# Memory tokens staged in scratch, pass-0 activations loaded ahead of the K/V projection, four io buffers

## The chip, the cores and the metric

The kernel runs on all 8 cores of one Trainium2 chip. Each core works on its own share of the data with its own copy of the program, and no core talks to another. The metric is the device time in microseconds of the slowest core.

## The reference, cut to what matters

The reference is one layer of a decoder for two groups of requests that share weights. Each core has one prompt of 2048 tokens, 16 sample requests of 8 tokens (128 rows), and 256 memory tokens, all 1024 wide:

```
mn = rms(mem_prompt, g_mem); mk = mn @ w_xk; mv = mn @ w_xv     # 256 tokens, both are outputs too
x += 0.5 * swiglu(rms(x) ; w_ffn1_in, w_ffn1_out)
x += concat(pool(z), conv(z)) @ w_mix_out      with z = rms(x) @ w_mix_in
x += cross_attn(rms(x), mk, mv)                # sample rows use cached keys and values
x += 0.5 * swiglu(rms(x) ; w_ffn2_in, w_ffn2_out)
y  = rms(x)
```

## The kernel before

The activations live on chip in transposed form: `xT` holds 8 blocks of 128 features by 1152 token columns in f32. The 2048 prompt tokens are done in two passes of 1024 columns (subs 0 and 1, of 512 columns each). The 128 sample rows are sub 2, at columns 1024 to 1151; they take part in the first half of the layer in pass 0 and in the second half in pass 1. `hT` (bf16) holds the normed activations, `U` (bf16) the inner ones of the FFN and of the mixer. `scr` is f32 scratch. It is 4224 elements wide in each partition, in three parts that the program calls `R0`, `R1` and `R2`; the mixer, the sample attention and the final norm use it.

A small planner, `Prog.add`, puts every instruction into the list of its engine in the order in which the Python code emits it. It derives the waits from named resources: a reader waits for the last writer, a writer for earlier readers and writers on other engines. No engine reorders its own list, so an instruction that waits holds up everything that stands behind it on the same engine. Plain loads and stores are issued by SP, weight loads (f32 in memory, cast to bf16 on the way) by POOL. Both kinds run on the core's 16 DMA engines, as two queues: q1 for SP, q0 for POOL.

Weights go through four slots `wsl` in the order of use. `prefetch(3)` issues the first four blocks, the two halves of `w_xk` and of `w_xv`, ahead of everything else. A later block is issued when the matmuls that read its slot are done.

`load_tokens` (L399) brings in 128 tokens: SP loads a 128 x 1024 f32 tile, 512 KB, into one of two `io` buffers. TensorE transposes its eight blocks into two PSUM banks. ScalarE copies the first bank and VectorE the second into `xT`. The buffer is free for the next load when the transposes have read it.

The opening runs in this order on every engine: two memory tiles into columns 0 to 255 of `xT`; the norm with gain 3 into `hT`; the key projection to `kTp`; sixteen 128 x 512 halves of K and V as rows, of which eight groups of matmuls, each copied by ScalarE into one of two `stg` buffers (L446) and stored by SP (L451); three state loads through the same `stg` buffers, with transposes and copies to `poolhT` and `convhT` (L460 to L474); then eight tiles of `x_p` and one of `x_s` with `load_tokens`; then the first norm of FFN 1 (L305 the squares, L205 the sum over features with a matrix of ones, L313 and L315 the reciprocal root, L321 the scaling).

At the end of pass 0 the two subs are finished one after the other. For each, `final_sub` (L555) norms into `yT` in `scr` (gain 5), transposes four tiles of 128 tokens back, copies each into an `io` buffer (ScalarE L570, VectorE L572) and lets SP store it to `y_p` (L578). Then four tiles of the next pass are loaded with `load_tokens` into the same columns of `xT`, and their norm for FFN 1 follows. Output tiles and loads take the `io` buffers in turn. At the end of pass 1 `final_sub` runs for subs 0, 1 and 2 without loads.

Of the kernel before, what the change touches and what calls it, by code (L numbers as in the profile page):

```python
# [6 lines left out]
F32 = mybir.dt.float32  # L7
BF16 = mybir.dt.bfloat16
AF = mybir.ActivationFunctionType
# [6 lines left out]
EPS = 1e-6  # L16
# [96 lines left out]
def build_program(dbg_stage=None, skip=()):  # L113
# [29 lines left out]
    def sb(name, shape, dt):  # L143
        return es.enter_context(nc.sbuf_tensor(name, list(shape), dt))
# [5 lines left out]
    sq = sb("sq", [128, 8, 512], BF16)  # L150
    rstd = [sb(f"rstd{i}", [128, 512], F32) for i in range(2)]
    sg = [sb(f"sg{i}", [128, 512], F32) for i in range(2)]
    io = [sb(f"io{i}", [128, 1024], F32) for i in range(2)]
    scr = sb("scr", [128, 3 * 1408], F32)
    scr2 = sb("scr2", [128, 3 * 1408], F32)
    scr_bf = scr.bitcast(BF16)
# [37 lines left out]
    def nb():  # L194
        b = bank_ctr[0] % 8
        bank_ctr[0] += 1
        return b

    def BK(b):
        return ("ps", b)  # L200
# [57 lines left out]
    def wres(b, npart):  # L258
        return [("w", b % 4, pi) for pi in range(npart)]
# [37 lines left out]
    def XR(si, k):  # L297
        return ("x", si, k)
# [27 lines left out]
    def norm(src, subs, gi, dst_t):  # L326
        for sub in subs:
            r, rr, xr = norm_sub(src, sub, gi, dst_t)
            norm_apply(src, sub, gi, (lambda k, c0, n: dst_t[:, k, c0:c0 + n]), r, rr, xr, (lambda si: [("hT", si)]))
# [64 lines left out]

    io_ctr = [0]

    def load_tokens(src_rows_ap, col0, si):
        i = io_ctr[0] % 2
        io_ctr[0] += 1  # L399
        buf = io[i]  # L400
        P.add("sp", (lambda e: e.dma_start(out=buf[:], in_=src_rows_ap)), writes=[("io", i)], dma_key=f"io{i}")
        for half in range(2):
            b = nb()
            for j in range(4):
                k = half * 4 + j
                transp(ps[b][:, j * 128:(j + 1) * 128], buf[:, k * 128:(k + 1) * 128], identf[:], [("io", i)], b)
            dstv = xT[:, half * 4:half * 4 + 4, col0:col0 + 128]
            srcv = ps[b][:, :].rearrange("p (j t) -> p j t", j=4)
            eng = "act" if half == 0 else "dve"
            if eng == "act":  # L410
                P.add("act", (lambda e, dstv=dstv, srcv=srcv: e.activation(out=dstv, in_=srcv, func=AF.Copy)),
                      reads=[BK(b)], writes=[XR(si, half * 4 + j) for j in range(4)])
            else:
                P.add("dve", (lambda e, dstv=dstv, srcv=srcv: e.tensor_copy(out=dstv, in_=srcv)),  # L414
                      reads=[BK(b)], writes=[XR(si, half * 4 + j) for j in range(4)])

    SUB_P = [(0, 0, 512), (1, 512, 512)]
    SUB_S = [(2, 1024, 128)]

    prefetch(3)  # L420
    if "kv" not in skip:
        for mc in range(2):
            load_tokens(mem[mc * 128:(mc + 1) * 128, :], mc * 128, 0)
        if "kv_norm" not in skip:
            norm(xT, [(0, 0, 256)], 3, hT)
        xk = sched["xk"]; xv = sched["xv"]
        for oc in (range(8) if "kv_kt" not in skip else []):
            blk = xk[oc // 4]
            sv = slot_view_blk(blk, 8, 512)
            b = nb()  # L430
            mm_group(ps[b][:, 0:256], [(sv[:, k, (oc % 4) * 128:(oc % 4 + 1) * 128], hT[:, k, 0:256]) for k in range(8)],
                     wres(blk, 1) + [("hT", 0)], b)
            P.add("act", (lambda e, b=b, oc=oc: e.activation(out=kTp[:, oc, :], in_=ps[b][:, 0:256], func=AF.Copy)),
                  reads=[BK(b)], writes=["kTp"])
        stg_ctr = [0]
        for (wb, dst_d, is_v) in (((xk, nk_p, False), (xv, nv_p, True)) if "kv_tok" not in skip else []):
            for mc in range(2):
                for cb in range(2):
                    blk = wb[cb]
                    sv = slot_view_blk(blk, 8, 512)  # L440
                    b = nb()
                    mm_group(ps[b][:, :], [(hT[:, k, mc * 128:(mc + 1) * 128], sv[:, k, :]) for k in range(8)],
                             wres(blk, 1) + [("hT", 0)], b)
                    i = stg_ctr[0] % 2
                    stg_ctr[0] += 1
                    P.add("act", (lambda e, b=b, i=i: e.activation(out=stg[i][:, :], in_=ps[b][:, :], func=AF.Copy)),  # L446
                          reads=[BK(b)], writes=[("stg", i)])
                    if is_v and "kv_vp" not in skip:
                        P.add("dve", (lambda e, i=i, mc=mc, cb=cb: e.tensor_copy(out=Vp[:, mc, cb * 512:(cb + 1) * 512], in_=stg[i][:, :])),
                              reads=[("stg", i)], writes=["Vp"])  # L450
                    P.add("sp", (lambda e, i=i, dst_d=dst_d, mc=mc, cb=cb: e.dma_start(  # L451
                        out=dst_d[mc * 128:(mc + 1) * 128, cb * 512:(cb + 1) * 512], in_=stg[i][:, :])),
                        reads=[("stg", i)], dma_key=f"stg{i}")
# [102 lines left out]
    def final_sub(sub):  # L556
        (si, c0, n) = sub
        pss_ = cur_pass[0]
        r, rr, xr = norm_sub(xT, sub, 5, None)
        norm_apply(xT, sub, 5, (lambda k, c0_, n_: yT3[:, k, 0:n_]), r, rr, xr, (lambda si_: ["R0", "R1", "R2"]))  # L560
        for tcn in range(n // 128):
            i = io_ctr[0] % 2
            io_ctr[0] += 1
            for half in range(2):
                b = nb()
                for j in range(4):
                    k = half * 4 + j
                    transp(ps[b][:, j * 128:(j + 1) * 128], yT3[:, k, tcn * 128:(tcn + 1) * 128], identf[:], ["R0", "R1", "R2"], b)
                if half == 0:
                    P.add("act", (lambda e, b=b, i=i: e.activation(out=io[i][:, 0:512], in_=ps[b][:, :], func=AF.Copy)), reads=[BK(b)], writes=[("io", i)])  # L570
                else:
                    P.add("dve", (lambda e, b=b, i=i: e.tensor_copy(out=io[i][:, 512:1024], in_=ps[b][:, :])), reads=[BK(b)], writes=[("io", i)])  # L572
            if si < 2:
                r0 = pss_ * 1024 + c0 + tcn * 128
                dst = y_p[r0:r0 + 128, :]
            else:
                dst = y_s[:, :]
            P.add("sp", (lambda e, i=i, dst=dst: e.dma_start(out=dst, in_=io[i][:, :])), reads=[("io", i)], dma_key=f"io{i}")  # L578
# [8 lines left out]
    for pss in range(2):  # L587
        cur_pass[0] = pss
        subs_a = SUB_P + (SUB_S if pss == 0 else [])
        subs_b = SUB_P + (SUB_S if pss == 1 else [])  # L590
        if "load" not in skip and not (pss == 1 and preload_next):
            for tcn in range(8):
                r0 = pss * 1024 + tcn * 128
                load_tokens(x_p[r0:r0 + 128, :], tcn * 128, tcn // 4)
            if pss == 0:
                load_tokens(x_s[:, :], 1024, 2)
# [362 lines left out]
```

How the kernel before makes its waits and increments, by code:

```python
    def emit(self, eng, handle, esem, dsem, final_wait=False):  # L86
        waited = {}
        for o in self.ops[eng]:
            for d in o.deps:
                if d.dma_key is not None:
                    sem = dsem[d.dma_key]
                    if d.dma_key in self.wait_all_keys:
                        val = 16 * self.dma_count[d.dma_key]
                    else:
                        val = 16 * d.dma_idx
                else:
                    sem = esem[d.eng]
                    val = d.sig_val
                key = id(sem)
                if waited.get(key, 0) < val:
                    handle.wait_ge(sem, val)
                    waited[key] = val
            ins = o.fn(handle)
            if o.dma_key is not None:
                ins.then_inc(dsem[o.dma_key], 16)
            elif o.signal:
                ins.then_inc(esem[eng], 1)
        if final_wait:
            for k, cnt in self.dma_count.items():
                handle.wait_ge(dsem[k], 16 * cnt)
```

## Time and profile before

| | us |
|---|---|
| median of 2 timed runs (1764.76 to 1765.17) | 1764.97 |
| the profiled execution, its own time | 1759.95 |
| span of its slowest core, first to last instruction | 1758.4 |
| spans of the 8 cores | 1752.9 to 1758.4 |
| TensorE busy in that span | 1509.1 |
| share of TensorE in the chain that ended last | 78% |

The rows further down are all from the slowest core, core 7, of the profiled execution. Times in them are microseconds from the start of the span. PE is TensorE, PEld its weight loads, DVE is VectorE, ACT is ScalarE, POOL is GpSimd, and SPq is the queue that issues SP's DMAs. Brackets at the end of a row of the timeline give the idle time before the instruction and what ended it.

### The profile page before, as it was taken

How to read it: one execution, taken by the hardware profiler on the slowest of the kernel's cores; microseconds unless marked ns; L12 is line 12 of the kernel's file. 1: busy time of each engine (PE TensorE's matmuls, PEld its weight loads, DVE VectorE, ACT ScalarE, POOL GpSimd, SP SyncE). 2: the span in 40 equal slices, each digit the busy share in tenths (PEclk: the TensorE clock that was granted, in tenths of full speed). 3: DMA queues.
4: the chain of work that ended last, by engine and by line, in shares of the span. 5: the costliest groups of instructions: out<-in, count | busy, mean ns of one | idle time of the engine just before them, and what ended most of it. 6: DMA issues, size and time to landing. Idle time of an engine off the chain costs nothing.

```text
span 1758.4 us, 23002 instructions; the slowest of 8 cores (1752.9 to 1758.4 us)
## 1 busy us (share of the span) xinstructions
PE 1509.1 (86%) x8516; PEld 758.1 (43%) x8516; DVE 611.9 (35%) x1046; ACT 411.3 (23%) x631; POOL 158.0 (9%) x191
## 2 busy tenths in 40 slices
PE   5269999986988889999953799998698889999984
PEld 3135554543444335545532344443243345454533
DVE  1042323246551442323343222224554252323243
ACT  2131010123124433231312210112312522011122
POOL 1000010010000011111100000001000000010000
PEclk9659999998999989999986799999899989999996
DMA  8913363552353269898982165547163334475502
GB/s 144 185 61 49 48 97 49 77 53 28 51 89 52 28 90 133 117 144 112 145 159 80 46 80 74 72 61 78 18 91 55 48 44 52 48 86 60 61 1 108
DMA packets 175178, 135.01 MB, mean 77 GB/s; under 512 B 29485, under 2 KB 160685, under 8 KB 175070
## 3 DMA queue, kind: packets, MB, share of 16 engines
q0 software_dynamic: 167344, 111.29, 49.3%
q1 hardware_dynamic: 7726, 22.26, 3.7%
q8 instruction: 71, 1.16, 0.3%
q14 instruction: 37, 0.30, 0.1%
HBM read 233.21 MB, written 11.60 MB: 139 GB/s over the span
## 4 chain that ended last, share of the span: by engine, by line
PE 78%; DVE 7%; DMA 6%; ACT 6%; issue 3%; SPq 0%; DVEq 0%; ACTq 0%; POOLq 0%
PE ps L205 75%; PE ps L209 3%; ACT sq L305 2%; DMA io<-x_p 2%; DVE hT L321 2%; DVE scr L659 1%; DVE scr L321 1%; DMA y_p<-io 1%; ACT ET L829 1%; DMA nv_p<-stg 1%; DMA scr<-ck 1%; DVE scr L733 1%; DMA io<-mem 1%; ACT rstd L313 1%; DMA stg<-st_pool 0%
## 5 line engine op out<-in xcount | busy, mean ns | idle before, releaser
L205 PE MATMUL ps<-hT,wsl 128*128 128x512 bf16 (+2 forms) x4800 | 914.1, 353 | 16.4 <-DVE hT L321 11.2
L205 PEld LDWEIGHTS ps<-hT,wsl 128*128 128x128 bf16 x4800 | 437.9, 99 | 486.9 <-issue 48.0
L205 PE MATMUL ps<-U,wsl 128*128 128x512 bf16 (+1 forms) x2080 | 387.5, 348 | 7.1 <-DVE U L744 5.3
L385 DVE TENSOR_TENSOR U<-ps,sg 128x512 bf16<-128x512 f32 (+1 forms) x220 | 134.6, 612 | 489.4 <-PE ps L205 469.9
L205 PEld LDWEIGHTS ps<-U,wsl 128*128 128x128 bf16 x2080 | 186.4, 98 | 203.6 <-issue 10.0
L383 ACT ACTIVATE sg<-ps 128x512 f32<-128x512 f32 (+1 forms) x220 | 117.4, 533 | 656.7 <-PE ps L205 656.6
L341 DVE SCALAR_TENSOR_TENSOR xT<-ps,xT 128x512 f32<-128x512 f32 (+1 forms) x240 | 144.7, 611 | 169.3 <-PE ps L205 167.0
L205 PE MATMUL ps<-sq,ones_n 128*128 128x512 bf16 (+2 forms) x208 | 64.0, 473 | 72.1 <-ACT sq L305 58.9
L321 DVE SCALAR_TENSOR_TENSOR hT<-xT,gains_sb,rstd 128x512 bf16<-128x512 f32 (+2 forms) x168 | 97.9, 657 | 72.8 <-ACT rstd L315 72.8
L305 ACT ACTIVATE sq<-xT 128x4096 bf16<-128x4096 f32 (+2 forms) x26 | 79.3, 3051 | 94.8 <-DVE xT L345 56.3
L209 PE MATMUL ps<-identf,io 128*128 128x128 f32 x152 | 35.2, 412 | 48.1 <-DMA io<-x_p 34.2
L345 DVE TENSOR_TENSOR xT<-ps,xT 128x512 f32<-128x512 f32 (+1 forms) x80 | 47.6, 610 | 66.2 <-PE ps L205 66.2
L205 PEld LDWEIGHTS ps<-sq,ones_n 128*128 128x128 bf16 x208 | 22.8, 122 | 108.7 <-issue 101.0
L252 POOL DMA_DIRECT2D wsl<-w_f1i x44 | 38.5, 883 | 252.0 <-PE ps L205 251.7
L252 POOL DMA_DIRECT2D wsl<-w_f2i x44 | 38.5, 885 | 246.1 <-PE ps L205 245.7
L209 PE MATMUL ps<-identf,scr 128*128 128x128 f32 x136 | 24.2, 360 | 33.2 <-DVE scr L321 33.2
L209 PEld LDWEIGHTS ps<-identf,io 128*128 128x128 f32 x152 | 29.0, 217 | 53.3 <-issue 53.3
L840 DVE TENSOR_TENSOR hT<-ps,rstd 128x512 bf16<-128x512 f32 x32 | 20.6, 686 | 84.3 <-ACT rstd L835 84.3
L313 ACT ACTIVATE rstd<-ps 128x512 f32<-128x512 f32 (+2 forms) x26 | 13.7, 528 | 113.6 <-PE ps L205 113.6
L414 DVE COPY xT<-ps 128x512 f32<-128x512 f32 x19 | 13.1, 692 | 77.1 <-PE ps L209 77.1
L252 POOL DMA_DIRECT2D wsl<-w_f1o x12 | 10.3, 856 | 316.3 <-PE ps L205 316.3
L209 PEld LDWEIGHTS ps<-identf,scr 128*128 128x128 f32 x136 | 23.0, 194 | 36.1 <-issue 36.1
(106 smaller groups left out, 611.4 us busy)
## 6 DMA issues: line engine op xcount, KB each, us to landing
wsl<-w_f1i POOLq DMA_DIRECT2D x44, 512.0 KB, 8.6
wsl<-w_f2i POOLq DMA_DIRECT2D x44, 512.0 KB, 10.9
io<-x_p SPq DMA_DIRECT2D x16, 512.0 KB, 4.1
wsl<-w_f1o POOLq DMA_DIRECT2D x8, 1024.0 KB, 8.8
scr<-ck POOLq DMA_DIRECT2D x16, 512.0 KB, 8.8
scr<-cv POOLq DMA_DIRECT2D x16, 512.0 KB, 7.2
wsl<-w_f2o POOLq DMA_DIRECT2D x8, 1024.0 KB, 12.2
y_p<-io SPq DMA_DIRECT2D x16, 512.0 KB, 2.8
```

What stands on the lines that cost most here:

```text
L205: P.add("pe", (lambda e, l=l, r=r, i=i: e.matmul(out_ap, lhsT=l, rhs=r, start=(i == 0), stop=(i == n - 1))), reads=reads, writes=[BK(b)])
L209: P.add("pe", (lambda e: e.transpose(out_ap, in_ap, ident_ap)), reads=reads + ["c_identf", "c_identb"], writes=[BK(b)])
L252: batch.append(P.add("pool", (lambda e, dst=dst, src=src: e.dma_start(out=dst, in_=src.rearrange("(k p) n -> p k n", p=128))), writes=[("w ...
L305: P.add("act", (lambda e: e.activation(out=sq[:, :, 0:n], in_=src[:, :, c0:c0 + n], func=AF.Square)), reads=xr, writes=["sq"])
L313: P.add("act", (lambda e: e.activation(out=r[:, 0:n], in_=ps[b][:, 0:n], func=AF.Ln, bias=EPS, scale=1.0)), reads=[BK(b)], writes=[rr])
L321: P.add("dve", (lambda e, k=k: e.scalar_tensor_tensor(out=dst(k, c0, n), in0=src[:, k, c0:c0 + n], scalar=gains[:, gi, k:k + 1], in1=r[:, ...
L341: P.add("dve", (lambda e, b=b, o=o, c0=c0, n=n: e.scalar_tensor_tensor(out=xT[:, o, c0:c0 + n], in0=ps[b][:, 0:n], scalar=0.5, in1=xT[:, o ...
L345: P.add("dve", (lambda e, b=b, o=o, c0=c0, n=n: e.tensor_tensor(out=xT[:, o, c0:c0 + n], in0=ps[b][:, 0:n], in1=xT[:, o, c0:c0 + n], op=AL ...
L383: P.add("act", (lambda e, bg=bg, n=n, s_=s_: e.activation(out=s_[:, 0:n], in_=ps[bg][:, 0:n], func=AF.Silu)), reads=[BK(bg)], writes=[("sg ...
L385: P.add("dve", (lambda e, bu=bu, n=n, s_=s_, jl=jl, c0=c0: e.tensor_tensor(out=U[:, jl, c0:c0 + n], in0=ps[bu][:, 0:n], in1=s_[:, 0:n], op ...
L659: P.add("dve", (lambda e, srcb=srcb, dstb=dstb, lo=lo, kstep=kstep: e.tensor_tensor(out=dstb[:, lo:1039], in0=srcb[:, lo:1039], in1=srcb[: ...
L840: P.add("dve", (lambda e, bo=bo, c=c, c0=c0, n=n, r=r: e.tensor_tensor(out=hT[:, c, c0:c0 + n], in0=ps[bo][:, 0:n], in1=r[:, 0:n], op=ALU. ...
```

## The change

There are three edits.

1. The `io` buffers become four (`NIO = 4`), in `load_tokens` and in `final_sub`.
2. The memory tiles are transposed into `memT`, the first 2048 columns of `scr`, with resource `R0`. They are normed from there into `U`, and both projections read `U` in place of `hT`. The instructions of that norm are the same in number and size.
3. The nine loads of pass 0 with their transposes and copies are emitted directly behind the two memory tiles, ahead of the memory norm, and leave their old place behind the state loads.

```diff
-    io = [sb(f"io{i}", [128, 1024], F32) for i in range(2)]
+    NIO = 4
+    io = [sb(f"io{i}", [128, 1024], F32) for i in range(NIO)]
...
-    def load_tokens(src_rows_ap, col0, si):
-        i = io_ctr[0] % 2
+    def load_tokens(src_rows_ap, col0, si, dst3=None, res_of=None):
+        dst3 = xT if dst3 is None else dst3
+        res_of = (lambda k: XR(si, k)) if res_of is None else res_of
+        i = io_ctr[0] % NIO
...
+    early_x = all(k not in skip for k in ("kv", "load"))
     prefetch(3)
     if "kv" not in skip:
+        memT = scr[:, 0:2048].rearrange("p (k t) -> p k t", k=8)
         for mc in range(2):
-            load_tokens(mem[mc * 128:(mc + 1) * 128, :], mc * 128, 0)
+            load_tokens(mem[mc * 128:(mc + 1) * 128, :], mc * 128, 0, dst3=memT, res_of=(lambda k: "R0"))
+        if early_x:
+            for tcn in range(8):
+                load_tokens(x_p[tcn * 128:(tcn + 1) * 128, :], tcn * 128, tcn // 4)
+            load_tokens(x_s[:, :], 1024, 2)
         if "kv_norm" not in skip:
-            norm(xT, [(0, 0, 256)], 3, hT)
+            P.add("act", (lambda e: e.activation(out=sq[:, :, 0:256], in_=memT[:, :, :], func=AF.Square)), reads=["R0"], writes=["sq"])
...
+            for k in range(8):
+                P.add("dve", (lambda e, k=k, r=r: e.scalar_tensor_tensor(
+                    out=U[:, k, 0:256], in0=memT[:, k, :], scalar=gains[:, 3, k:k + 1], in1=r[:, 0:256], op0=ALU.mult, op1=ALU.mult)),
+                    reads=["R0", ("rstd", 0), "c_gains"], writes=[("U", 0)])
...
         for tcn in range(n // 128):
-            i = io_ctr[0] % 2
+            i = io_ctr[0] % NIO
...
-        if "load" not in skip and not (pss == 1 and preload_next):
+        if "load" not in skip and not (pss == 1 and preload_next) and not (pss == 0 and early_x):
```

## Rows read from the trace of the kernel before

**Rows 1.** The page, parts 1 and 4: busy share, and the chain by engine.

```profile
PE 1509.1 (86%) x8516; PEld 758.1 (43%) x8516; DVE 611.9 (35%) x1046; ACT 411.3 (23%) x631; POOL 158.0 (9%) x191
...
PE 78%; DVE 7%; DMA 6%; ACT 6%; issue 3%; SPq 0%; DVEq 0%; ACTq 0%; POOLq 0%
```

**Rows 2.** The timeline, 0 to 60 us: start, duration, engine, line, op.

```profile
3.38 0.90 SPq L401 DMA_DIRECT2D io<-mem  x2
...
15.10 1.94 PE L209 MATMUL ps<-identf,io 128*128 128x128 f32 x8 [0.95 <-DMA io<-mem]
...
17.93 1.91 ACT L305 ACTIVATE sq<-xT 128x2048 bf16<-128x2048 f32 x1 [1.05 <-DVE xT L414]
...
26.34 8.98 PE L205 MATMUL ps<-hT,wsl 128*128 128x256 bf16 x64 [4.49 <-DVE hT L321]
```

**Rows 3.** The timeline, 60 to 130 us.

```profile
71.76 25.25 SPq L401 DMA_DIRECT2D io<-x_p  x8
...
78.68 0.28 ACT L474 ACTIVATE convhT<-ps 128x128 f32<-128x128 f32 x1 [0.55 <-PE ps L209]
...
104.56 3.61 ACT L305 ACTIVATE sq<-xT 128x4096 bf16<-128x4096 f32 x1
```

**Rows 4.** DMA queues, 8 to 12 us: packets, MB, share of 16 engines.

```profile
q1 hardware_dynamic: 202, 0.76, 62.4%
q0 software_dynamic: 232, 0.24, 43.5%
```

**Rows 5.** DMA queues, 20 to 26 us, the same columns.

```profile
q0 software_dynamic: 1000, 1.01, 115.9%
```

**Rows 6.** The chain that ended last, 0 to 180 us: start, duration, what.

```profile
71.76 8.56 DMA io<-x_p
...
82.58 3.55 DMA io<-x_p
```

**Rows 7.** DMA issues of the whole span: KB each, median us to landing.

```profile
io<-x_p SPq DMA_DIRECT2D x16, 512.0 KB, 4.1
...
y_p<-io SPq DMA_DIRECT2D x16, 512.0 KB, 2.8
...
wsl<-w_xv POOLq DMA_DIRECT2D x2, 1024.0 KB, 29.3
...
io<-mem SPq DMA_DIRECT2D x2, 512.0 KB, 9.8
...
nv_p<-stg SPq DMA_DIRECT2D x4, 256.0 KB, 7.7
```

**Rows 8.** The timeline of the pass boundary, 895 to 994 us.

```profile
902.66 5.96 PE L209 MATMUL ps<-identf,scr 128*128 128x128 f32 x32 [7.20 <-DVE scr L321]
...
905.53 6.31 SPq L578 DMA_DIRECT2D y_p<-io  x4
...
913.15 8.69 SPq L401 DMA_DIRECT2D io<-x_p  x4
918.01 3.42 PE L209 MATMUL ps<-identf,io 128*128 128x128 f32 x16 [9.38 <-DMA io<-x_p]
...
927.99 0.69 DVE L414 COPY xT<-ps 128x512 f32<-128x512 f32 x1 [0.66 <-PE ps L209]
...
951.90 5.25 PE L209 MATMUL ps<-identf,scr 128*128 128x128 f32 x32 [7.05 <-DVE scr L321]
...
978.03 0.69 DVE L414 COPY xT<-ps 128x512 f32<-128x512 f32 x1 [2.40 <-PE ps L209]
```

**Rows 9.** The timeline of the end, 1660 to 1759 us.

```profile
1716.19 5.40 PE L209 MATMUL ps<-identf,scr 128*128 128x128 f32 x32 [8.70 <-DVE scr L321]
...
1725.04 3.61 ACT L305 ACTIVATE sq<-xT 128x4096 bf16<-128x4096 f32 x1
...
1739.54 5.66 PE L209 MATMUL ps<-identf,scr 128*128 128x128 f32 x32 [7.07 <-DVE scr L321]
...
1747.35 1.05 ACT L305 ACTIVATE sq<-xT 128x1024 bf16<-128x1024 f32 x1
```

More of the change, by code:

```diff
@@ L406, in load_tokens @@
                 transp(ps[b][:, j * 128:(j + 1) * 128], buf[:, k * 128:(k + 1) * 128], identf[:], [("io", i)], b)
-            dstv = xT[:, half * 4:half * 4 + 4, col0:col0 + 128]
+            dstv = dst3[:, half * 4:half * 4 + 4, col0:col0 + 128]
             srcv = ps[b][:, :].rearrange("p (j t) -> p j t", j=4)
@@ L411, in load_tokens @@
                 P.add("act", (lambda e, dstv=dstv, srcv=srcv: e.activation(out=dstv, in_=srcv, func=AF.Copy)),
-                      reads=[BK(b)], writes=[XR(si, half * 4 + j) for j in range(4)])
+                      reads=[BK(b)], writes=[res_of(half * 4 + j) for j in range(4)])
             else:
                 P.add("dve", (lambda e, dstv=dstv, srcv=srcv: e.tensor_copy(out=dstv, in_=srcv)),
-                      reads=[BK(b)], writes=[XR(si, half * 4 + j) for j in range(4)])
+                      reads=[BK(b)], writes=[res_of(half * 4 + j) for j in range(4)])
     SUB_P = [(0, 0, 512), (1, 512, 512)]
     SUB_S = [(2, 1024, 128)]
+    early_x = all(k not in skip for k in ("kv", "load"))
     prefetch(3)
     if "kv" not in skip:
+        memT = scr[:, 0:2048].rearrange("p (k t) -> p k t", k=8)
         for mc in range(2):
-            load_tokens(mem[mc * 128:(mc + 1) * 128, :], mc * 128, 0)
-        if "kv_norm" not in skip:
-            norm(xT, [(0, 0, 256)], 3, hT)
+            load_tokens(mem[mc * 128:(mc + 1) * 128, :], mc * 128, 0, dst3=memT, res_of=(lambda k: "R0"))
[3 more added lines that the diff above has]
+            load_tokens(x_s[:, :], 1024, 2)
+        if "kv_norm" not in skip:
+            P.add("act", (lambda e: e.activation(out=sq[:, :, 0:256], in_=memT[:, :, :], func=AF.Square)), reads=["R0"], writes=["sq"])
+            b = nb()
+            mm_group(ps[b][:, 0:256], [(ones_n[:], sq[:, k, 0:256]) for k in range(8)], ["sq", "c_ones_n"], b)
+            r = rstd[0]
+            P.add("act", (lambda e, b=b, r=r: e.activation(out=r[:, 0:256], in_=ps[b][:, 0:256], func=AF.Ln, bias=EPS, scale=1.0)),
+                  reads=[BK(b)], writes=[("rstd", 0)])
+            P.add("act", (lambda e, r=r: e.activation(out=r[:, 0:256], in_=r[:, 0:256], func=AF.Exp, scale=-0.5)), reads=[("rstd", 0)], writes=[("rstd", 0)])
+            for k in range(8):
+                P.add("dve", (lambda e, k=k, r=r: e.scalar_tensor_tensor(
+                    out=U[:, k, 0:256], in0=memT[:, k, :], scalar=gains[:, 3, k:k + 1], in1=r[:, 0:256], op0=ALU.mult, op1=ALU.mult)),
+                    reads=["R0", ("rstd", 0), "c_gains"], writes=[("U", 0)])
         xk = sched["xk"]; xv = sched["xv"]
@@ L430, in build_program @@
             b = nb()
-            mm_group(ps[b][:, 0:256], [(sv[:, k, (oc % 4) * 128:(oc % 4 + 1) * 128], hT[:, k, 0:256]) for k in range(8)],
-                     wres(blk, 1) + [("hT", 0)], b)
+            mm_group(ps[b][:, 0:256], [(sv[:, k, (oc % 4) * 128:(oc % 4 + 1) * 128], U[:, k, 0:256]) for k in range(8)],
+                     wres(blk, 1) + [("U", 0)], b)
             P.add("act", (lambda e, b=b, oc=oc: e.activation(out=kTp[:, oc, :], in_=ps[b][:, 0:256], func=AF.Copy)),
@@ L441, in build_program @@
                     b = nb()
-                    mm_group(ps[b][:, :], [(hT[:, k, mc * 128:(mc + 1) * 128], sv[:, k, :]) for k in range(8)],
-                             wres(blk, 1) + [("hT", 0)], b)
+                    mm_group(ps[b][:, :], [(U[:, k, mc * 128:(mc + 1) * 128], sv[:, k, :]) for k in range(8)],
+                             wres(blk, 1) + [("U", 0)], b)
                     i = stg_ctr[0] % 2
```

## Prediction

> **What bounds the kernel now.** I read the page first. TensorE is busy for 86% of the span and makes 78% of the chain that ended last [rows 1]. This change touches no dense stage, so it can only win or lose in the stretches where the chain leaves TensorE. I looked for those in the timeline, and three matter here. The first is the opening. TensorE begins with the memory tiles, and the key projection starts at 26.34 [rows 2]. The sixteen K/V halves, their stores and the state loads then run until the last state copy at 78.68. The nine activation tiles follow, and the first squares of FFN 1 start only at 104.56 [rows 3]. Between the two there is nothing but loads, short transposes and copies. The second stretch is the pass boundary, where each sub is normed, transposed out, stored, loaded and normed again while TensorE has no other work [rows 8]. The third is the end, where three final norms run in a row [rows 9]. At the boundary the reader is to see loads that start late, at 913.15, because they wait for the same two buffers as the stores, so that TensorE stood idle for 9.38 us until 918.01 [rows 8].
>
> **Part 1: the loads leave their old place.** Behind the change ScalarE's queue holds the first squares right after the copy to `convhT`, and their data are long there. The gap that closes is 104.56 - (78.68 + 0.28) = 25.6 us [rows 3]. The first FFN weights are issued during the K/V matmuls, as before, so their lead shrinks by the same 25.6 us. The activation load issued at 71.76 took 8.56 us and the one at 82.58 only 3.55 [rows 6], so q0's backlog was gone a few us after the last state copy, and two whole norm steps still stand before the first FFN matmul: I cost this at nothing. If it were wrong, FFN 1 would wait a few us once.
>
> **Part 2: the loads at their new place.** Now nine tiles stand ahead of the memory norm in every queue. TensorE must transpose them all before the sum of squares, ScalarE copies them before the memory squares, and VectorE copies them before the scaling. SP issues them ahead of the K/V stores, which need the projection anyway. So the K/V work starts later by the time from the second memory tile to the ninth activation tile, and everything down to the last state copy moves with it. Let r be the time from one tile's landing to the next's. Before, the second memory tile's transposes started at 15.10 and the key projection at 26.34, 11.24 us later. Of these, 1.05 us were ScalarE waiting for VectorE's copy of the memory tile [rows 2], which is done early now, so 10.2 us remain. The projection then starts at 15.1 + 9r + 10.2, and it is late by 9r - 1.0. The opening changes by 9r - 1.0 - 25.6 = 9r - 26.6 us. It breaks even at r = 2.96 us: the change has to load a tile faster than that, and it does so while the weights of K and V are coming in.
>
> What is r? In 8 to 12 us q1 moved 0.76 MB, almost all of it the memory tiles, while q0 moved 0.24 MB beside it [rows 4]. That is 0.19 MB/us, or 2.76 us for a tile of 0.524 MB. Four buffers keep at least two loads queued, so the first wait of a load (issue to landing of a memory tile is 9.8 us [rows 7]) overlaps with its neighbours. A buffer's round is then some 9.8 + 1.94 (transposes, [rows 2]), over four 2.9 us a tile. The fast end is 2.2, the transposes of one tile (1.94) and a short wait, since TensorE does nothing else meanwhile. Slower values are 3.55, the load time behind the backlog in the old place [rows 6], where two buffers were in use, and 4.28, if two loads share a turn of 8.56 us. I take 2.8, nearest to the row that has the same two queues full at the same time. The opening changes by 9 x 2.8 - 26.6 = -1.4 us. The ends are -6.8 (r = 2.2) and +11.9 (r = 4.28), with +5.4 at 3.55.
>
> The weights of K and V must also be there. q0 alone moves 1.01 MB in 6 us [rows 5], 0.168 MB/us, and 4.2 MB of bf16 weights landed by about 34 [rows 7]. Beside q1 it moves 0.06 MB/us [rows 4]. About 0.94 MB were in by 15 us; 25 us beside the loads add 1.5; the last 1.8 take 11 us more, so the last block is in near 51. The key projection would start at 50.5 and reads only the first 2.1 MB. `w_xv` is wanted some 14 us later. So no wait, with little to spare for the key half if q0 gets less.
>
> The Trainium skill (DMA: Bandwidth & Descriptors, Queues, rings and completion order) says that each DMA engine goes round between the queue rows and drains a whole packet from one before it switches. By that rule a plain load behind a weight backlog waits out a turn of q0, and with one load per turn the opening would lose; the second rival works this out from rows. The two memory tiles were served in one stretch, so the trace so far agrees with it only in part.
>
> **Part 3: memory tiles in `scr`, norm into `U`.** It is the same instructions on other addresses. The two copies of a memory tile now carry one resource, so VectorE's copy waits for ScalarE's, at most 0.7 us each, long before the squares read them: nothing. It does free columns 0 to 255 of `xT` and `hT`, without which the early loads couldn't run. `U` and `scr` are not used by anybody else before FFN 1 and the mixer. Nothing, on either side.
>
> **Part 4: four buffers at the pass boundary.** For sub 0 TensorE makes four output tiles in 5.96 us, 1.49 each, and the first store is issued 2.87 us after the start, at 905.53 [rows 8]. With a buffer for every tile the stores go out at 905.5, 907.0, 908.5 and 910.0. They land 2.8 us later [rows 7], and each landing releases a load: 908.3 to 912.8, where the first load was issued at 913.15 before. A load takes 4.1 us in the median [rows 7] and 4.86 from issue to its transposes on this spot (913.15 to 918.01 [rows 8]). The last transposes could start at 912.8 + 4.86 = 917.7. Paced by 1.94 us of transposes per tile from 913.2 they start at 919.0. VectorE's last copy follows some 2.0 us behind (1.94 of transposes and the start of the copy), at 919.7 to 921.0 in place of 927.99: 7.0 to 8.3 us. For sub 1 the same sum from 951.90, with 1.31 us per tile, gives 968.4 to 970.3 in place of 978.03: 7.7 to 9.6 us. All that follows is a serial chain of norm steps, so it is kept. I take 7.6 + 7.9 = 15.5. The low end is that only the first load starts earlier (4.8 us) and the others land at the pace of before, because stores and loads share the engines: 9.6 for both. The high end is 17.9.
>
> **Part 5: four buffers at the end.** ScalarE's fourth copy can follow the seventh of eight banks: 1716.19 + 7/8 x 5.40 + 0.7 = 1721.6, and the squares of sub 1 stand right behind it, at 1725.04 before: 3.4 us. For sub 1: 1739.54 + 7/8 x 5.66 + 0.7 = 1745.2 against 1747.35: 2.1 us [rows 9]. Between the first two TensorE also has sub 2's last projection to do, which could eat the first gain; so 5.5, with a low end of 2.1.
>
> **Sum.** -1.4 - 15.5 - 5.5 = -22.4 us. The profiled execution takes 1759.95, which gives 1737.6. The timed median stands 5.0 us above it, and from 1764.97 the sum gives 1742.6. I predict 1742.6, 1.3% below.
>
> **The rivals.**
> - **Loads slow beside the weights**: r between 3.55 and 4.28. For it speaks the wait of 8.56 us of the first load under a backlog [rows 6]. Against it speaks the rate of the two queues side by side [rows 4]. The opening loses 5.4 to 11.9 in place of winning 1.4: 1749 to 1756.
> - **One load for each turn of the weight queue.** A store or load alone under the backlog took 7.7 to 8.6 us [rows 6, 7]. With about 8 us a tile from 15 us on, q0 gets 0.11 MB/us between turns, its last 3.3 MB take 30 us, and 3.7 tiles are in by 45. The other 5.3 come at 3.5 each, until 63. That is r = 5.3 on average and +21.3 for the opening. With the boundary at its low end (9.6) and 5.5 at the end it makes +6.2: 1771, slower than before. It decides from r = 5.3 up at the full gains, 4.6 at the low end. Against it: both memory tiles landed within 3 us of one another.
> - **The boundary is bound by the DMA engines**, part 4 at its low end: -1.4 - 9.6 - 5.5, 1748.5.
> - **Fast tiles**: r = 2.2 and part 4 near its high end: -6.8 - 17.0 - 5.5, 1736.
> - **The change doesn't do what it says**: the loads are issued early but the gap after the states stays, since something else holds the first squares. Then part 2 costs 24 us and part 1 gives nothing: 1768. I see no such holder in the queues.
>
> **How the numbers follow.** Chances: forecast 0.57, slow loads 0.19, one load per turn 0.05, boundary bound 0.09, fast tiles 0.08, no effect at the old place 0.02. The range from 1734 to 1757 takes in all but the two cases above 1760 and the far edges of the others. About 2% (35 us) is what a measurement of this kernel can tell from no change. Faster by that needs the high end of every part and more, 0.04; slower by that, 1800, is out of reach of every case named, 0.02; within 2%, 0.94.
>
> **What would show it.** In the changed profile: ten or eleven `io` loads in the first 40 us with tiles 2.8 us apart; the key projection near 50; the first squares of FFN 1 within 1 us behind the last state copy, near 103; no wait of K/V matmuls for weights; four `y_p` stores at each boundary 1.5 us apart with no copy waiting for a store, and each boundary some 7.7 us shorter; a tail some 5 us shorter. The prediction is wrong if r is over 4, if FFN 1 waits for `w_f1i`, or if loads and stores at the boundary slow each other so much that their landings stretch beyond 7 us.

## The result, and the profile after

The changed kernel takes 1744.21 us in the median of all its timed runs, against 1765.17 for the kernel before, where 1742.6 was forecast. Three of the timed runs of each kernel were in a slower state, with a lower granted clock on some of the cores, and the ratios of this document leave such runs out. The ratio is 0.9878, with a 95% interval of 0.9865 to 0.9892: 21 to 22 us or 1.2% faster. The profiled execution took 1742.48 us; its slowest core spans 1740.9, which is 17.5 less than the span of before.

The first view is the page of the changed kernel, parts 1 and 4, which answer to [rows 1]:

```profile
PE 1505.1 (86%) x8516; PEld 757.0 (43%) x8516; DVE 612.1 (35%) x1046; ACT 411.2 (24%) x631; POOL 158.0 (9%) x191
...
PE 79%; DVE 6%; ACT 6%; DMA 5%; issue 3%; SPq 0%; DVEq 0%; ACTq 0%; POOLq 0%
```

The counts of instructions are the same on every engine, and so nearly are the busy times. Nothing became cheaper. What went is idle time. The timeline of the changed kernel, 0 to 125 us (core 6, the slowest), shows the opening as [rows 2, 3] do for the kernel before:

```profile
4.33 24.88 SPq L404 DMA_DIRECT2D io<-x_p  x8
...
16.68 1.94 PE L210 MATMUL ps<-identf,io 128*128 128x128 f32 x8 [1.25 <-DMA io<-mem]
...
40.38 1.94 PE L210 MATMUL ps<-identf,io 128*128 128x128 f32 x8 [0.57 <-DMA io<-x_s]
...
50.46 9.93 PE L206 MATMUL ps<-U,wsl 128*128 128x256 bf16 x64 [4.49 <-DVE U L442]
...
105.00 0.28 ACT L493 ACTIVATE convhT<-ps 128x128 f32<-128x128 f32 x1 [1.87 <-PE ps L210]
105.17 3.61 ACT L306 ACTIVATE sq<-xT 128x4096 bf16<-128x4096 f32 x1
```

From the second memory tile (16.68) to the ninth activation tile (40.38) are 23.7 us: a tile every 2.63 us. The key projection starts at 50.46 instead of 26.34. Everything behind it is late by that, and the first squares of FFN 1 follow the last state copy at once. They start at 105.17 where they started at 104.56 before. On these two cores the move of the loads is an even exchange.

The two profiles have different slowest cores, and core 7 happened to be the earliest of all in the kernel before. The timelines of all eight cores give a better mean. Start of the first squares of FFN 1, us:

```
core            0       1       2       3       4       5       6       7     mean
before     107.02  108.50  108.88  105.81  109.07  104.87  107.76  104.56   107.06
changed    102.08  105.57  103.18  105.22  101.42  103.73  105.17  101.60   103.50
```

So the opening is 3.6 us shorter in the mean. The key projection, read in the same way, starts at 27.2 in the mean before and at 49.5 after, 22.3 later; the gap between the last state copy and the squares, which went, was 26.1.

The DMA queues of the changed kernel in 20 to 36 us, with packets, MB and share of 16 engines, answer to [rows 4]:

```profile
q1 hardware_dynamic: 846, 3.10, 60.1%
q0 software_dynamic: 1058, 1.07, 47.8%
```

That is 0.194 MB/us for the activations beside 0.067 for the weights, where [rows 4] had 0.19 and 0.06.

The timeline of the pass boundary of the changed kernel, 870 to 980 us, against [rows 8]:

```profile
901.71 5.83 PE L210 MATMUL ps<-identf,scr 128*128 128x128 f32 x32 [7.20 <-DVE scr L322]
...
904.59 4.47 SPq L597 DMA_DIRECT2D y_p<-io  x4
...
909.57 3.76 SPq L404 DMA_DIRECT2D io<-x_p  x4
914.95 6.03 PE L210 MATMUL ps<-identf,io 128*128 128x128 f32 x32 [7.42 <-DMA io<-x_p]
...
921.97 3.62 ACT L306 ACTIVATE sq<-xT 128x4096 bf16<-128x4096 f32 x1 [0.73 <-DVE xT L417]
...
945.10 6.31 PE L210 MATMUL ps<-identf,scr 128*128 128x128 f32 x32 [7.05 <-DVE scr L322]
...
953.01 4.42 SPq L404 DMA_DIRECT2D io<-x_p  x4
959.62 5.89 PE L210 MATMUL ps<-identf,io 128*128 128x128 f32 x32 [8.21 <-DMA io<-x_p]
...
966.39 3.62 ACT L306 ACTIVATE sq<-xT 128x4096 bf16<-128x4096 f32 x1 [0.63 <-DVE xT L417]
```

No copy waits for a store any more. The squares of the kernel before, in the timeline of [rows 8], are

```profile
928.77 3.62 ACT L305 ACTIVATE sq<-xT 128x4096 bf16<-128x4096 f32 x1 [1.05 <-DVE xT L414]
...
978.81 3.62 ACT L305 ACTIVATE sq<-xT 128x4096 bf16<-128x4096 f32 x1 [1.05 <-DVE xT L414]
```

From the first transposes of a sub to the squares of the next pass are 20.26 and 21.29 us. Before they were 26.11 and 26.91 (from 902.66 and 951.90): 5.85 and 5.62 us saved, 11.5 together. In the mean of the eight cores the two stretches together fell from 51.9 to 39.7 us, by 12.2. TensorE still stands idle for 7.4 and 8.2 us; of these, 5.4 and 6.6 are the way of the first load from its issue to its transposes. SP's queue alone, 908.6 to 914 us, shows what the first load stood behind:

```profile
908.73 0.33 SPq L597 DMA_DIRECT2D y_p<-io  x1
909.57 3.76 SPq L404 DMA_DIRECT2D io<-x_p  x4
```

It is the fourth store, not the landing of the first: SP's only waits from 903 to 909.9 us are for VectorE's copies of the output tiles.

The timeline of the end, 1680 to 1742 us, against [rows 9]:

```profile
1704.71 5.40 PE L210 MATMUL ps<-identf,scr 128*128 128x128 f32 x32 [8.71 <-DVE scr L322]
...
1710.62 3.61 ACT L306 ACTIVATE sq<-xT 128x4096 bf16<-128x4096 f32 x1
...
1714.48 1.89 PE L206 MATMUL ps<-sq,ones_n 128*128 128x512 bf16 x8 [1.69 <-ACT sq L306]
...
1723.43 6.26 PE L210 MATMUL ps<-identf,scr 128*128 128x128 f32 x32 [7.06 <-DVE scr L322]
...
1729.96 1.05 ACT L306 ACTIVATE sq<-xT 128x1024 bf16<-128x1024 f32 x1
...
1737.85 0.33 SPq L597 DMA_DIRECT2D y_s<-io  x1
```

Two rows of the same stretch of the kernel before, which [rows 9] do not hold:

```profile
1728.90 3.57 PE L205 MATMUL ps<-sq,ones_n 128*128 128x512 bf16 x8 [2.32 <-ACT sq L305]
...
1755.24 0.33 SPq L578 DMA_DIRECT2D y_s<-io  x1
```

From the first of these transposes to the last store's issue are 33.14 us (1704.71 to 1737.85), against 39.05 before (1716.19 to 1755.24): 5.9 us saved, 5.8 in the mean of the eight cores. The three means together, -3.6 - 12.2 - 5.8 = -21.6 us, account for the whole difference: the mean span of the eight cores fell by 21.3 us (1756.7 to 1735.4).

### The profile page after: what moved, and what is told of

Same layout as the page of the kernel before. It is cut to its first block, busy times and chain, and to the rows that moved or that the text cites. A ratio compares the mean times of both kernels' runs of the same rounds, so it can differ in the third digit from the quotient of the medians.

```text
span 1740.9 us, 23005 instructions; the slowest of 8 cores (1729.2 to 1740.9 us)
## 1 busy us (share of the span) xinstructions
PE 1505.1 (86%) x8516; PEld 757.0 (43%) x8516; DVE 612.1 (35%) x1046; ACT 411.2 (24%) x631; POOL 158.0 (9%) x191
## 4 chain that ended last, share of the span: by engine, by line
PE 79%; DVE 6%; ACT 6%; DMA 5%; issue 3%; SPq 0%; DVEq 0%; ACTq 0%; POOLq 0%
PE ps L206 76%; PE ps L210 3%; ACT sq L306 2%; DMA io<-x_p 2%; DVE hT L322 1%; DVE scr L678 1%; DVE scr L322 1%; DMA nv_p<-stg 1%; ACT ET L848 1%; DMA scr<-ck 1%; DVE scr L752 1%; ACT rstd L314 1%; DMA io<-x_s 1%; ACT rstd L853 0%; ACT rstd L316 0%
## 5 line engine op out<-in xcount | busy, mean ns | idle before, releaser
L206 PE MATMUL ps<-hT,wsl 128*128 128x512 bf16 (+1 forms) x4736 | 905.5, 354 | 11.0 <-DVE hT L322 6.1
L206 PEld LDWEIGHTS ps<-hT,wsl 128*128 128x128 bf16 x4736 | 430.5, 99 | 480.0 <-issue 42.5
L206 PE MATMUL ps<-U,wsl 128*128 128x512 bf16 (+2 forms) x2144 | 396.9, 348 | 9.8 <-DVE U L763 5.3
L206 PEld LDWEIGHTS ps<-U,wsl 128*128 128x128 bf16 x2144 | 193.7, 99 | 208.5 <-issue 12.4
L322 DVE SCALAR_TENSOR_TENSOR hT<-xT,gains_sb,rstd 128x512 bf16<-128x512 f32 (+1 forms) x160 | 94.6, 666 | 87.4 <-ACT rstd L316 87.4
L306 ACT ACTIVATE sq<-xT 128x4096 bf16<-128x4096 f32 (+1 forms) x25 | 77.4, 3097 | 92.4 <-DVE xT L346 55.7
L210 PE MATMUL ps<-identf,io 128*128 128x128 f32 x152 | 30.8, 381 | 39.1 <-DMA io<-x_p 23.7
L253 POOL DMA_DIRECT2D wsl<-w_f1i x44 | 38.5, 883 | 277.1 <-PE ps L206 276.7
L253 POOL DMA_DIRECT2D wsl<-w_f2i x44 | 38.5, 884 | 246.1 <-PE ps L206 245.7
L314 ACT ACTIVATE rstd<-ps 128x512 f32<-128x512 f32 (+1 forms) x25 | 13.3, 533 | 109.3 <-PE ps L206 109.2
L253 POOL DMA_DIRECT2D wsl<-w_mi x26 | 22.8, 892 | 155.1 <-PE ps L206 155.1
## 6 DMA issues: line engine op xcount, KB each, us to landing
wsl<-w_f2i POOLq DMA_DIRECT2D x44, 512.0 KB, 10.8
```

The costliest lines, as they stand in the source:

```text
L206: P.add("pe", (lambda e, l=l, r=r, i=i: e.matmul(out_ap, lhsT=l, rhs=r, start=(i == 0), stop=(i == n - 1))), reads=reads, writes=[BK(b)])
L210: P.add("pe", (lambda e: e.transpose(out_ap, in_ap, ident_ap)), reads=reads + ["c_identf", "c_identb"], writes=[BK(b)])
L253: batch.append(P.add("pool", (lambda e, dst=dst, src=src: e.dma_start(out=dst, in_=src.rearrange("(k p) n -> p k n", p=128))), writes=[("w ...
L306: P.add("act", (lambda e: e.activation(out=sq[:, :, 0:n], in_=src[:, :, c0:c0 + n], func=AF.Square)), reads=xr, writes=["sq"])
L314: P.add("act", (lambda e: e.activation(out=r[:, 0:n], in_=ps[b][:, 0:n], func=AF.Ln, bias=EPS, scale=1.0)), reads=[BK(b)], writes=[rr])
L322: P.add("dve", (lambda e, k=k: e.scalar_tensor_tensor(out=dst(k, c0, n), in0=src[:, k, c0:c0 + n], scalar=gains[:, gi, k:k + 1], in1=r[:, ...
```

## The experiments

The theory on trial is that the four buffers make the gain, and that the early loads pay only because of them. Ratios are to the kernel before on the same chip, with 95% intervals; where a time stands beside one, it is the ratio times 1765.

| kernel | ratio | interval |
|---|---|---|
| the change | 0.9878 | 0.9865 to 0.9892 |
| four buffers only | 0.9865 | 0.9848 to 0.9882 |
| early loads, two buffers from the first pass on | 0.9977 | 0.9966 to 0.9989 |
| early loads, two buffers everywhere | 1.0080 | 1.0059 to 1.0102 |
| the change, V weights late | 0.9896 | 0.9879 to 0.9914 |
| the change, K/V rows in scratch | 0.9746 | 0.9725 to 0.9767 |
| four buffers, K/V rows in scratch, transposes behind K/V | 0.9763 | 0.9740 to 0.9787 |
| four buffers, next pass loaded ahead | 0.9738 | 0.9720 to 0.9755 |
| the last two together | 0.9633 | 0.9618 to 0.9648 |
| the change, FFN 1 weights late | 0.9777 | 0.9760 to 0.9795 |
| the change, K/V rows in scratch, next pass loaded ahead | 0.9612 | 0.9591 to 0.9633 |

**Four buffers and nothing else.** The loads of pass 0 stay in their old place.

```diff
-    io = [sb(f"io{i}", [128, 1024], F32) for i in range(2)]
+    io = [sb(f"io{i}", [128, 1024], F32) for i in range(4)]
...
-            i = io_ctr[0] % 2
+            i = io_ctr[0] % 4
```

> The kernel before with four io buffers and nothing else. Theory A (the four buffers make the gain, the move of the loads is an even exchange): the two pass boundaries together 11 to 12 us shorter and the end 6 us shorter, as in the changed kernel, and at the old place the last activation tile some 1.6 us earlier, since four loads are queued behind the first wait; about 19 us in all, a ratio near 0.989. Theory B (the move of the loads makes the gain): 5 us or less, a ratio of 0.997 or more. Theory C (both are needed at once, the buffers pay at the boundary only half): near 10 us, 0.994.

Measured: 0.9865, the whole gain of the change. The timeline of this kernel, 0 to 130 us (core 6):

```profile
84.13 0.28 ACT L474 ACTIVATE convhT<-ps 128x128 f32<-128x128 f32 x1 [0.22 <-PE ps L209]
...
100.82 1.06 PE L209 MATMUL ps<-identf,io 128*128 128x128 f32 x8 [1.63 <-DMA io<-x_s]
102.04 3.61 ACT L305 ACTIVATE sq<-xT 128x4096 bf16<-128x4096 f32 x1
```

Between the last state copy and the squares lie 17.6 us here, 25.6 before [rows 3]: four loads stand in the queue together. Over the eight cores the squares start at 100.4 us in the mean, 6.6 earlier than before and 3.1 earlier than in the change; 1.6 was expected. The two boundary stretches take 42.0 us together in the mean, 9.8 less than before, where 11 to 12 was expected. They are 2.3 longer than in the change, which has the same code there; the cause of that was not followed. The end is 5.9 shorter, as expected. Theory A stands on the total. The move adds nothing to the four buffers; it may cost 2 us, though the two intervals overlap.

**Four buffers in the opening alone.**

```diff
-        i = io_ctr[0] % NIO
+        i = io_ctr[0] % nio[0]      # 4 in the opening, 2 from the first pass on
```

> The changed kernel, but from the first pass on output tiles and loads go round two io buffers again; only the opening has four. Theory A: the opening changes by 9r - 26.6 with r near 2.65 us, so by 0 to -3 us, and the boundary and the end stay as they were: 1763 to 1766, a ratio of 0.998 to 1.0. Theory B: the whole gain is here, near 1745, 0.988.

Measured: 0.9977, 4 us faster. That is less than a fifth of the gain, so theory B is out. The boundary and the end stay within 1 us of those before, in the mean of the eight cores.

**Early loads with two buffers everywhere.**

```diff
-    NIO = 4
+    NIO = 2
```

> The changed kernel with two io buffers everywhere. Theory A (r is set by the wait of each load under the weight backlog, over the number of buffers): a load takes some 9.8 us and its transposes 2, so r is 6 us until the weights are in at about 45 us and 3.5 after that, 5 on average. The key projection starts near 70 and the kernel takes about 1783, a ratio of 1.010. Rival (r is set by the rate of the two DMA queues, buffers or not): r stays 2.7 to 3, the key projection starts near 52, and the time is that of the kernel before.

Measured: 1.0080, 14 us slower than before and 36 us slower than the change. The timeline of this kernel, 0 to 130 us (core 4), shows why:

```profile
15.46 1.94 PE L210 MATMUL ps<-identf,io 128*128 128x128 f32 x8 [0.61 <-DMA io<-mem]
...
23.37 1.94 PE L210 MATMUL ps<-identf,io 128*128 128x128 f32 x8 [5.97 <-DMA io<-x_p]
...
26.10 1.94 PE L210 MATMUL ps<-identf,io 128*128 128x128 f32 x8 [0.78 <-DMA io<-x_p]
...
34.47 1.94 PE L210 MATMUL ps<-identf,io 128*128 128x128 f32 x8 [6.42 <-DMA io<-x_p]
...
37.45 1.94 PE L210 MATMUL ps<-identf,io 128*128 128x128 f32 x8 [1.04 <-DMA io<-x_p]
...
68.14 9.34 PE L206 MATMUL ps<-U,wsl 128*128 128x256 bf16 x64 [4.49 <-DVE U L442]
```

Tiles come in pairs, and each pair costs one wait: 23.37, 34.47, 45.50 for the first of each. That is 11.1 us for two tiles, 5.5 each, and 4.7 on average over nine. By 9r - 26.6 the opening loses 16 us; 14 were lost. Beside the weights a load lands 8.6 us after its issue in the median here (15 to 44 us), and 8.5 in the change (4 to 32 us), though twice as many are queued there. With 1.94 of transposes a buffer's round is 10.5 us, which is 5.3 a tile over two buffers and 2.6 over four. So it is the number of loads in the queue that sets r in these two kernels. The rate of the queues alone doesn't; whether it would with more than four buffers no run shows.

**The V weights behind the activations.**

```diff
-    prefetch(3)
+    prefetch(1)
...
             load_tokens(x_s[:, :], 1024, 2)
+        prefetch(3, rd=[XR(1, 7)])
```

> The changed kernel, but the weights of V (half of the 4.2 MB) are issued only when the eighth activation tile has been copied. Theory A (beside the weights the DMA rate sets r): r is as before up to about 25 us, where the weights of K are in, and 2.2 after that; the key projection starts 2 to 3 us earlier, and the weights of V land about 47, ahead of their use at 64: 2 to 3 us faster than the changed kernel, a ratio near 0.986. Rival (transposes and the landing of each load set r): no change against 0.988. Rival on the other side: the V weights come too late, the K/V stage waits for them, and the run is slower than the changed kernel.

Measured: 0.9896, no faster than the change. The DMA queues of this kernel, 20 to 36 us:

```profile
q1 hardware_dynamic: 919, 3.36, 62.9%
q0 software_dynamic: 938, 0.95, 43.0%
```

The activations got 0.21 MB/us in place of 0.194, because the K weights still stood in the queue for all of this time (the second block landed 35.2 us after its issue, near 38.5). The key projection starts at 48.63 instead of 50.46, and half of that is a memory tile that landed 1 us earlier; in the mean of the eight cores it starts at 49.1 instead of 49.5. The last state copy then comes at 105.73: the stage behind the projection is 2.6 us longer than in the change, so the little that was won did not arrive. The expectation (2 to 3 us) missed. What an earlier projection is worth depends on what ends the next stage, which the following kernels ask.

**K/V rows in the second scratch.** The eight row tiles get places of their own (`kvs(i)` is 512 columns of `scr2`), and the state loads are issued ahead of the K/V stores; the two edits were not tried apart.

```diff
-                    P.add("act", (lambda e, b=b, i=i: e.activation(out=stg[i][:, :], in_=ps[b][:, :], func=AF.Copy)),
-                          reads=[BK(b)], writes=[("stg", i)])
+                    P.add("act", (lambda e, b=b, i=i: e.activation(out=kvs(i), in_=ps[b][:, :], func=AF.Copy)),
+                          reads=[BK(b)], writes=[("kvs", i)])
...
             load_tokens(x_s[:, :], 1024, 2)
+        state_loads()
```

> The changed kernel, but the eight K/V row tiles go to eight places of their own in the second scratch (unused until the mixer) in place of two stg buffers, and the three state loads are issued ahead of the K/V stores. Theory A (behind the move the opening is bound by stores and state loads that take turns with the weight queue through two buffers, not by the activation loads): the first squares of FFN 1 follow the K/V matmuls at 50.5 + 23.9 + 3, near 77 in place of 105, 28 us less: about 1716, a ratio of 0.972. Rival (the first weights of FFN 1 become the bound): they are issued at 66 and 73 and took 21 us in the median, so TensorE would wait for them at 96 or later and less than 20 us would be won, 0.977 or more.

Measured: 0.9746, 1720 us. The timeline of this kernel, 0 to 130 us (core 2):

```profile
74.22 0.98 PE L210 MATMUL ps<-identf,stg 120*128 120x120 f32 x8
...
76.03 3.64 ACT L306 ACTIVATE sq<-xT 128x4096 bf16<-128x4096 f32 x1
...
95.19 35.00 PE L206 MATMUL ps<-hT,wsl 128*128 128x512 bf16 x198
```

The squares start at 76.03 where 77 was expected; over the eight cores the mean is 75.0, 28.5 us earlier than in the change, and TensorE goes into FFN 1 at 95.19 with no wait for weights. In the changed kernel the opening is thus bound by the stores and state loads that pass two `stg` buffers. The activation loads, in either place, were not the larger part. The whole run gained some 23 us of these 28.5. The mean span of the eight cores is 25.2 shorter; the boundary stretches, whose code is the same, gave back 2.3 (42.0 against 39.7), and where the rest went was not followed.

**The same, with the transposes behind K/V.** Built on the order of before, with four buffers. Only the issue of four activation loads is moved up.

```diff
+        pre_x = [issue_load(x_p[t * 128:(t + 1) * 128, :]) for t in range(2)]
+        state_loads()
+        pre_x += [issue_load(x_p[t * 128:(t + 1) * 128, :]) for t in range(2, 4)]
```

> The kernel before with four io buffers, K/V rows in the second scratch and early state loads, and only the issue of the first four activation loads moved up; their transposes stay behind the K/V matmuls. Theory A: the K/V stage runs from 26 to 50 as before, four tiles are there by then, five more come at 2.6 us each behind a first wait of 8.5 under the backlog of FFN weights, so the first squares come near 74 to 77: as good as the kernel with all nine tiles ahead, about 1713 to 1716, 0.971. Rival (transposing early is what made the opening short): 10 us or more slower than that.

Measured: 0.9763, the same within the intervals. The squares start at 81.31 on the slowest core, 4 to 7 us later than expected. The timeline of this kernel, 30 to 70 us (core 0), has the reason:

```profile
32.82 3.65 PE L205 MATMUL ps<-hT,wsl 128*128 128x256 bf16 x32 [0.56 <-DMA wsl<-w_xk]
...
50.38 7.16 PE L205 MATMUL ps<-wsl,hT 128*128 128x512 bf16 x23 [5.28 <-DMA wsl<-w_xv]
```

The loads took DMA time from the weights, and here the K/V matmuls run early enough to feel it: 5.28 us of waiting for `w_xv`. In the change the same delay of the weights (for `w_xv` 29.3 us in the median from issue to landing before [rows 7], 40.6 here and 43.8 in the change) is hidden behind the transposes.

**The next pass loaded ahead.** The kernel before with four buffers; the four tiles of a sub are loaded into the second scratch long before the boundary, and those of sub 1 as soon as sub 0's are transposed.

```diff
-                    for tcn_ in range(4):
-                        r0_ = 1024 + c0_ + tcn_ * 128
-                        load_tokens(x_p[r0_:r0_ + 128, :], c0_ + tcn_ * 128, si_)
+                    nx_take(sub)
+                    if si_ == 0:
+                        nx_issue(SUB_P[1])
...
+                nx_issue(SUB_P[0])
```

> The kernel before with four io buffers, and the next pass's tiles at the boundary are loaded into the second scratch ahead of time, so that no load waits for a store. Theory A (what is left at the boundary is the landing of a store and then of a load, 7.4 and 8.2 us of TensorE idle in the changed kernel's trace): 14 to 15 us less than with four buffers alone, about 1727, 0.978. Rival (the two copying engines set the pace there): 5 us or less, 0.984.

Measured: 0.9738, 22 us less than four buffers alone, where 14 to 15 were expected. The timeline of this kernel, 850 to 985 us:

```profile
899.40 9.27 PE L209 MATMUL ps<-identf,scr 128*128 128x128 f32 x64 [7.20 <-DVE scr L321]
...
909.64 3.62 ACT L305 ACTIVATE sq<-xT 128x4096 bf16<-128x4096 f32 x1 [0.71 <-DVE xT L607]
...
932.26 9.89 PE L209 MATMUL ps<-identf,scr 128*128 128x128 f32 x64 [7.05 <-DVE scr L321]
...
943.05 3.62 ACT L305 ACTIVATE sq<-xT 128x4096 bf16<-128x4096 f32 x1 [0.64 <-DVE xT L607]
```

The stretches are 10.2 and 10.8 us. In the mean of the eight cores they take 20.9 together, against 42.0 with four buffers alone. The expectation counted only TensorE's idle time. But the 64 transposes now run as one batch in 9.27 us, 145 ns each, where 32 took 5.83 and another 32 took 6.03 in the change. The granted clock tells why. This batch starts at 0.50 of full speed, the lower level of 1.2 GHz (899.4 to 903.4), and its last 3.3 us run at 1.00. In the change both batches start at 0.50, in 901.7 to 905.7 and again, after the idle time, in 914.95 to 918.95. So what bounds a boundary with four buffers is the wait for a load that is issued behind four stores, and a second batch of transposes that starts behind it at the lower clock. The copying engines don't.

**The last two together.** The edits of the kernel with the transposes behind K/V and of the one with the next pass loaded ahead:

```diff
+        pre_x = [issue_load(x_p[t * 128:(t + 1) * 128, :]) for t in range(2)]
...
+                nx_issue(SUB_P[0])
```

> The last two together. If they are as independent as they look, the gains add: 1765 - 50 - 15, about 1700, a ratio of 0.963. If the weight queue becomes the bound of the opening, 10 us less is won, 0.969.

Measured: 0.9633, 1700 us: the gains add.

**The FFN 1 weights late.** The changed kernel; the first four blocks of FFN 1 wait for the last state copy.

```diff
-    prefetch(sched["xv"][1] + 3)
...
               reads=[BK(b)], writes=["convhT"])
+    prefetch(sched["xv"][1] + 3, rd=["convhT"])
```

> The changed kernel, but the first four weight blocks of FFN 1 are issued only behind the last state copy, so that no weight backlog runs beside the K/V stores and the state loads. Theory A (each store and state load waits about 5 us behind the weight queue, which is what fills 74 to 105 us): the stores take 2.6 us as the first ones do, the last state copy comes near 82 in place of 105, the first weights land by 93, ahead of the first matmul of FFN 1 at 101: about 20 us less than the changed kernel, 1724, a ratio of 0.977. Rival (the two stg buffers and the copies set that pace, not the backlog): 5 us or less. Rival on the other side: FFN 1 waits for its weights and gives most of it back.

Measured: 0.9777, 1726 us. The DMA issues of the changed kernel come first (KB each, median us from issue to landing):

```profile
nv_p<-stg SPq DMA_DIRECT2D x4, 256.0 KB, 7.9
...
stg<-st_pool SPq DMA_DIRECT2D x2, 240.0 KB, 6.8
```

and then those of this kernel:

```profile
nv_p<-stg SPq DMA_DIRECT2D x4, 256.0 KB, 2.2
...
stg<-st_pool SPq DMA_DIRECT2D x2, 240.0 KB, 3.7
```

A V store takes 2.2 us without a backlog of weights and 7.9 with one. The timeline of this kernel, 40 to 130 us:

```profile
82.46 0.28 ACT L491 ACTIVATE convhT<-ps 128x128 f32<-128x128 f32 x1 [1.41 <-PE ps L210]
82.63 3.61 ACT L306 ACTIVATE sq<-xT 128x4096 bf16<-128x4096 f32 x1
83.40 7.00 POOL L253 DMA_DIRECT2D wsl<-w_f1i  x8 [77.42 <-ACT convhT L491]
...
102.30 27.96 PE L206 MATMUL ps<-hT,wsl 128*128 128x512 bf16 x151 [0.22 <-issue]
```

The last state copy comes at 82.46, 22.5 us earlier than in the change, with the same two buffers and the same queue of SP. The weights issued at 83.40 are there when FFN 1 wants them at 102.30. So the stage is long only where a backlog of weights and two buffers for the stores meet: without the backlog the squares come at 81.8 in the mean of the eight cores, without the shared buffers at 75.0, and with both at 103.5. The Trainium skill (DMA: Bandwidth & Descriptors, Queues, rings and completion order) says that a DMA engine drains a whole packet of one row before it goes to the next; the two medians of the V store, 2.2 and 7.9 us, fit it, though no row shows a single packet's turn.

**The change with K/V rows in scratch and the next pass loaded ahead.** Both edits as shown above, on the changed kernel:

```diff
+        state_loads()
...
+                nx_issue(SUB_P[0])
```

> The changed kernel with K/V rows in the second scratch, early state loads, and the next pass's tiles loaded ahead into the second scratch at the boundary. The opening of the first gave 25 us less than the changed kernel, the boundary 23.5 less than four buffers alone. They don't touch each other: 1719 - 24, about 1695, a ratio of 0.961; with its opening some 5 us shorter than where the transposes stay behind the K/V matmuls, it should be 2 to 4 us faster than the other combined kernel (0.9633).

Measured: 0.9612, 1697 us, the fastest kernel of the study, though not surely ahead of the other combination (0.9633). Here the first matmul of FFN 1 runs at 94.85, there at 101.02, each on its slowest core.

## Why the prediction was right

**The size and its parts.** Forecast were -1.4 for the opening, -15.5 for the boundary and -5.5 for the end, -22.4 in all. Measured in the mean of the eight cores were -3.6, -12.2 and -5.8, -21.6 in all. The mechanism was right, but that the total came out so close is in part luck: the boundary gave 3.3 less than forecast and the opening 2.2 more.

**The opening.** The form 9r - 1.0 held: r was 2.8 in the forecast and 2.63 on the slowest core. That the key projection was forecast for 50.5 and came at 50.46 is luck as well, since the second memory tile came 1.6 us late on that core and the faster tiles made up for it; the mean is 49.5. The rate of the plain queue beside the weights, read from four microseconds of the trace of before [rows 4], is the rate seen in 20 to 36 us of the change. But it is not shown to be the reason for r: the other estimate of the prediction, a buffer's round over four, gives 2.6 with the measured 8.5 us to landing, and with two buffers it gives 5.3 where 5.5 was measured, which the rate doesn't. The end beyond which the change would lose was real as well: with two buffers r is 4.7 and the kernel is slower than before. The gap behind the last state copy closed as forecast. FFN 1 didn't wait for its weights. The last V block was forecast for 51 and landed near 51.5; in the kernel before it lands near 37, not by the 34 that I read from a median.

**The base of the sum.** I took everything from core 7, whose squares came first of the eight, 2.5 us ahead of the mean. The gap, which is what the sum uses, differs less: 25.6 on core 7 and 26.1 in the mean. The projection was late by 22.3 us in the mean and not by the forecast 24.2, and that is most of the 2.2 us. One core's rows are enough for a mechanism, but a sum of 2 us should be made from all of them.

**The boundary: the mis-sized term.** I took 15.5 for two subs; the runs showed 12.2 in the mean, inside the ends of 9.6 and 17.9. The step that was off is that each store's landing releases a load, the first at 908.3. In the program's order all four stores stand in SP's list ahead of the first load, and my own times had the fourth store at 910.0. From the first store's issue to the first load's are 5.0 us in the mean of both subs on all cores (904.59 to 909.57 in the rows above), where I had 2.8. The load then took 5.2 us to its transposes, 5.4 in those rows, not 4.86. The four tiles' transposes gave some of it back: 5.9 us together, not 1.94 each. The landing of the stores was not at fault. On seven of the eight cores its median at the boundary is 2.7 or 2.8 us with four buffers too; only on core 6, whose rows are shown, it is 3.7. The loads do land later, in 5.4 to 6.5 us in the median where it was 3.5 to 4.5 before. That four of them share the engines fits; no run measured it apart.

**The end: a right sum from wrong parts.** 5.5 was forecast and 5.8 measured, 5.9 on the slowest core. The first squares gained 2.9 us there (8.85 to 5.91 behind the transposes), not 3.4, and the second 1.3 (7.81 to 6.53), not 2.1. The other 1.7 the forecast didn't have: the sum of squares at 1714.48 took 1.89 us at a granted clock of 1.00, where the same eight matmuls took 3.57 at 0.50 before (1728.90). TensorE was busy without a pause from 1704.71 to 1712.79 ahead of it, where it had stood idle three times before, for 1.39, 0.30 and 2.32 us, as the output copies, and the squares behind them, waited for stores. The projection of sub 2 took nothing from the gain.

**The rivals.** Slow loads and one load per turn did not occur in the change. The long wait beside a weight backlog exists nevertheless: 8.5 us for a load in either place, shared by all loads that are queued together, by four in the change and by two with two buffers, and 7.9 us for a V store in the K/V stage, where two buffers leave room for two. In that last place it was part of the kernel before already; I saw the 7.7 us stores [rows 7] and used them only as a price for a rival.

**What I would not have said beforehand.** The move of the loads, the larger part of the code, has no gain of its own once there are four buffers (0.9865 without it, 0.9878 with it).

## What to carry to other kernels

In this kernel plain loads beside a backlog of weight loads paid their wait per group of queued transfers, not per transfer. So count how many can be queued together before moving transfers into a busy stretch: the same move gained 4 us with four buffers and lost 14 with two. Where buffers pass both stores and loads, look at the chain store, load, first use before anything else, and in the order of the issuing queue too: a load that stands behind the stores in the list waits for their issue, even when its buffer is free. A region that is idle at that time may take either side out of the chain.

## What the runs showed of the hardware

A 256 KB store took 2.2 us with no weight loads in flight and 7.9 us beside four blocks of them (medians of the slowest cores; 2.0 to 2.3 and 7.1 to 9.0 over the eight). Plain loads of 512 KB beside the weights landed 8.5 us after their issue with four buffers and 8.6 with two, in the median of the slowest cores, and so came every 2.6 us with four and every 5.5 with two. The weight queue fell from 0.168 MB/us alone [rows 5] to 0.067 MB/us beside them (counted in bf16 bytes, of which it reads twice as many), and the last V block landed some 51 us after the start instead of 37. I had expected the rates, but not that holding the weights back for 17 us would make the whole run 18 us faster (0.9777 against 0.9878).
